# Moving a small norm between the halves of one matmul unit, and a weight split behind two others, in a two-block transformer kernel

## What is computed

```python
# compressed keys of the first attention (nsa)
kc = rms_norm(compress(rope(heads(nkc, G), pos), ...), nsa_kc_norm)   # silu(flat @ w1) @ w2, then norm
vc = compress(heads(nvc, G), cmp_v_pe, cmp_v_w1, cmp_v_w2)
g_nsa = jax.nn.sigmoid(heads(ngate, NSA_HEADS))

# second attention (mla): latents, expanded to queries, keys and values of 8 heads
q_b = (rms_norm(cq, mla_cq_norm) @ w_uq).reshape(B, S, MLA_HEADS, MLA_QK_DIM)
kv_b = (rms_norm(ckv, mla_ckv_norm) @ w_ukv).reshape(B, S, MLA_HEADS, MLA_NOPE_DIM + MLA_V_DIM)
q_b, k_b = rms_norm(q_b, mla_q_norm), rms_norm(k_b, mla_k_norm)       # then rope on the last 64 of 192
```

## Time and profile before

| | |
|---|---|
| median of 3 runs | 1177.66 us (1174.51 to 1179.42) |
| the profiled execution | 1175.0 us, span 1173.7 |
| busy share of the span | TensorE 96%, DVE 64%, ACT 50%, POOL 4% |
| chain that ended last | TensorE 86%, DVE 6%, ACT 4% |
| mean granted TensorE clock | 0.981 of full speed |

### The profile page before, as it was taken

How to read it: one execution, slowest core, us unless ns; L and a number is a source line. 1 busy time by engine, 2 the same in 40 slices (tenths; PEclk the granted TensorE clock), 3 DMA queues, 4 the chain that set the end, 5 groups by cost and what they waited for, 6 DMA issues and landing times.

```text
span 1173.7 us, 19229 instructions
## 1 busy us (share of the span) xinstructions
PE 1126.4 (96%) x7766; PEld 1022.1 (87%) x7766; DVE 755.3 (64%) x1411; ACT 590.5 (50%) x1043; POOL 48.6 (4%) x48
## 2 busy tenths in 40 slices
PE   8999898989899999999998999999999999999998
PEld 7988788888679999888987799998888978999986
DVE  3567486787668778775666666665455566666644
ACT  3365274454556666435344564444465256544542
POOL 0250010000000000101000000000000000000000
PEclk9999899899899999999998999999999999999999
DMA  8954834454135555564632375555544324655450
GB/s 319 390 189 176 339 144 180 154 204 146 40 139 198 183 181 187 215 243 175 235 111 73 119 261 180 179 180 174 185 162 144 108 77 162 204 187 180 131 193 36
DMA packets 30796, 207.81 MB, mean 177 GB/s; under 512 B 3539, under 2 KB 4051, under 8 KB 7156
## 3 DMA queue, kind: packets, MB, share of 16 engines
q1 hardware_dynamic: 30708, 206.58, 49.4%
HBM read 205.52 MB, written 1.05 MB: 176 GB/s over the span
## 4 chain that ended last, share of the span: by engine, by line
PE 86%; DVE 6%; ACT 4%; issue 2%; DMA 1%; SPq 0%; POOL 0%; ACTq 0%; DVEq 0%
PE ps L393 49%; PE ps L1642 19%; PE ps L627 3%; PE ps L411 2%; DVE wlo L352 1%; ACT whi L345 1%; DMA raw<-wa 1%; PE ps L2250 1%; PE ps L2282 1%; PE ps L1340 1%; DVE tm L566 1%; PE ps L816 1%; PE ps L1767 1%; PE ps L1418 1%; PE ps L1142 1%
## 5 line engine op out<-in xcount | busy, mean ns | idle before, releaser
L352 DVE TENSOR_TENSOR wlo<-raw,whi 128x1024 fp32r<-128x1024 f32 (+2 forms) x328 | 372.3, 1177 | 257.1 <-ACT whi L345 256.7
L393 PE MATMUL ps<-H_h,whi 128*128 128x256 f32 x1552 | 446.1, 287 | 0.0
L393 PE MATMUL ps<-H_l,whi 128*128 128x256 f32 x1552 | 440.5, 284 | 0.0
L393 PE MATMUL ps<-H_h,wlo 128*128 128x256 f32 x1552 | 440.5, 284 | 0.0
L345 ACT ACTIVATE whi<-raw 128x1024 fp32r<-128x1024 f32 (+2 forms) x328 | 315.3, 1011 | 176.5 <-PE ps L1642 110.8
L393 PEld LDWEIGHTS ps<-H_h,whi 128*128 128x128 f32 x1552 | 299.4, 193 | 3.9 <-issue 3.3
L393 PEld LDWEIGHTS ps<-H_l,whi 128*128 128x128 f32 x1552 | 299.3, 193 | 0.7 <-issue 0.5
L393 PEld LDWEIGHTS ps<-H_h,wlo 128*128 128x128 f32 x1552 | 299.1, 193 | 0.0
L1642 PE MATMUL ps<-whi,gl_h 128*128 128x512 f32 x264 | 105.6, 400 | 0.5 <-DVE wlo L352 0.5
L1642 PE MATMUL ps<-wlo,gl_h 128*128 128x512 f32 x264 | 104.6, 396 | 0.0
L1642 PE MATMUL ps<-whi,gl_l 128*128 128x512 f32 x264 | 104.6, 396 | 0.0
(11 more groups left out here) (446 smaller groups left out, 1548.9 us busy)
## 6 DMA issues: line engine op xcount, KB each, us to landing
raw<-f SPq DMA_DIRECT2D x44, 1024.0 KB, 4.9
raw<-win SPq DMA_DIRECT2D x27, 1024.0 KB, 5.0
raw<-ada SPq DMA_DIRECT2D x24, 1024.0 KB, 4.9
raw<-up SPq DMA_DIRECT2D x22, 1024.0 KB, 4.8
raw<-g SPq DMA_DIRECT2D x20, 1024.0 KB, 4.9
raw<-pw SPq DMA_DIRECT2D x12, 1024.0 KB, 4.9
raw<-down SPq DMA_DIRECT2D x10, 1024.0 KB, 6.0
raw<-wa SPq DMA_DIRECT2D x4, 1024.0 KB, 10.0
```

Source lines behind the costliest of these rows:

```text
L352: dve.tensor_tensor(wlo[j % NS][:, a:b], raw_of(key)[:, a:b], whi[j % NS][:, a:b].bitcast(F32), ALU.subtract).then_inc(w_lo.hit(key, half), 1)
L393: ins_ = pe.matmul(bank[:, m * 256:(m + 1) * 256], wt[a][:, kt * w + col + m * 128:kt * w + col + m * 128 + 128], act[b][:, k0 + kt, :], s ...
```

## The change

The norm's step on TensorE is issued between the two halves of ("uq", 0) instead of behind both. On ACT it comes behind the copy of the first half, instead of behind that of the second, and on DVE ahead of the gate's two steps and the rotation of `kr`, instead of behind the low split of ("uq", 2). Separately, ACT's and DVE's splits of ("ukv", 1) move from ahead of the hidden layer of the compressed values to behind part 1 of the four parts: on ACT behind the copy of that part, on DVE behind the norm of part 0. One line changes its indentation only.

```diff
@@ latent_pe
                 mm_fm(pe, ("uq", i), cqn, normed("vs") if (i, half) == (0, 0) else held, b, half * 256,
                       done=unit.hit("uq", i) if half else half_done.hit("uq", i))
+                if (i, half) == (0, 0):
+                    key_norm_pe(pe)
...
             if i == 0:
-                key_norm_pe(pe)
                 ada_sums_pe(pe, 8)
@@ latent_act
         for i in range(3):
-            if i == 1:
-                key_norm_act(act)
             if i == 2:
                 cmp_row_act(act, 1)
             next_hi(act, ("uq", i))
...
                 act.activation(dst, v2(where["uq", i, half][:]), ACT.Copy).then_inc(ev_act.hit("uq", i, half), 1)
-        next_hi(act, ("ukv", 0))
+                if (i, half) == (0, 0):
+                    key_norm_act(act)
         hidden_act(act, 1)
...
             act.activation(mk[:, 2 * half:2 * half + 2, :], v2(where["ukv", 0, half][:]), ACT.Copy).then_inc(
                 ev_act.hit("ukv", 0, half), 1)
+            if half == 1:
+                next_hi(act, ("ukv", 0))
         next_hi(act, ("ukv", 1))
@@ latent_dve
         next_lo(dve, ("uq", 0))
+        key_norm_dve(dve)
         dve.wait_ge(*gt_exp())
...
         next_lo(dve, ("uq", 1))
-        key_norm_dve(dve)
         mod_dve(dve, 8)
...
-        next_lo(dve, ("ukv", 0))
         hidden_dve(dve, 1)
         for half in range(4):
             mq_rope_dve(dve, half)
             if half:
                 mq_norm_dve(dve, half - 1)
+            if half == 1:
+                next_lo(dve, ("ukv", 0))
             if half == 2:
                 value_dve(dve)
```

More of the change, by code:

```diff
@@ L1089, in latent_pe @@
                 mm_fm(pe, ("uq", i), cqn, normed("vs") if (i, half) == (0, 0) else held, b, half * 256,
-                      done=unit.hit("uq", i) if half else half_done.hit("uq", i))
+                        done=unit.hit("uq", i) if half else half_done.hit("uq", i))
+                if (i, half) == (0, 0):
+                    key_norm_pe(pe)
             if i == 1:
```

## The result

The changed kernel's median is 1168.48 us (1167.19 to 1171.81, 5 runs) against 1177.66 for the kernel before (1174.34 to 1179.42, 5 runs). The ratio is 0.9947, 95% interval [0.9923, 0.9971]: faster, by 0.3 to 0.8%. The medians lie 9.2 us apart, the means 8.1, and the ratio says 6.2, with an interval of 3.4 to 9.1: five runs each don't tell the gain more closely. The profiled execution took 1167.19 us, span 1165.9, which is 7.8 less than the span of before. The forecast was 1170.1 (1166.1 to 1174.2).

What follows compares the result with a forecast made beforehand. TensorE, busy 96% of the span, was taken to bound the kernel, so only its stalls count. Terms 3.95 + 2.66 + 0.95 = 7.6 us off the median 1177.66 gave 1170.1 us, range 1166.1 to 1174.2.

Steps and rivals of the forecast that it cites:

- Part 1: Norm moved between halves of ("uq", 0): wait ahead of L581 gone, 3.95 us, and slow clock behind it, 2.66 us.
- The split into terms: At L581: 3.95 us idle time, plus 2.66 us slow clock (L581 0.79, L816 0.87, L393 1.00).
- the tightest place: L816 of ("cv1", 2): load landed at 133.0, TensorE comes to it at 133.55, 0.5 us of cover.
- Part 2: Splits of ("ukv", 1) moved: wait ahead of L1142 gone, 1.44 us, less a new wait of 0.5, net 0.95.
- The price at key part 3: Statistics of key part 3: DVE 1.1 us late, so TensorE gets a new wait of 0.5 us.
- the gain comes off either: Whole kernel: the 7.6 us come off the profiled execution, 1175.0, or the median of the runs, 1177.66.
- I see nothing at a fixed time to wait for: Behind the changed stretch: everything is tied to TensorE's progress and loads to buffer read-out, so all follows 7.6 us earlier.
- the prediction's last sign of being wrong: Anywhere in the kernel: the clock falls at a place where it doesn't fall in the kernel before.
- Only the first part pays: Rival: ACT or DVE, carrying the moved split, give its gain back; gain 6.6 us, time 1171.1; chance 0.08.
- The idle time comes back, the clock does not: Rival: at L581 only the idle time is regained; total gain 4.9 us, time 1172.8; chance 0.07.
- The attention stage swallowed nothing: Rival at 220 to 230 us: DVE-bound attention leaves at most some 2 us, 1175.7; chance 0.08 including no effect.
- The slower case: Rival at L816 of ("cv1", 2): load late; landing 20 us after issue gives +7.3, 1185.0; chance 0.03.

Runs made afterwards that it cites:

- filling the wait: Kernel before plus eight matmuls with unread result between L875 and the L581 pair, against the kernel before: timed +2.5 us, ratio 1.0022.
- the repetition: The unaltered changed kernel once more, on the chip that timed the variants, against the kernel before: timed -5.2 us, ratio 0.9957.
- the split only: Kernel before with only both splits of ("ukv", 1) moved behind part 1 of the four parts: timed +2.5 us, ratio 1.0022.
- DVE's step only: Kernel before with only DVE's norm multiply moved, ahead of the low split of ("uq", 2): timed -0.1 us, ratio 0.9998.
- norm on TensorE and ACT only: Kernel before with only TensorE's and ACT's norm steps moved, DVE's multiply left behind the low split: timed +0.1 us, ratio 1.0003.
- norm only: Kernel before with the norm's three steps moved, both splits of ("ukv", 1) left in place: timed -1.6 us, ratio 0.999.

## Why the prediction came out

**Part 1.** The mechanism was as forecast. L875 was forecast at 130.5, `kcn` at 132.2, L581 at 133.1; they came at 130.44, 131.71 to 131.96 and 132.81, all in a run whose stage begins 0.2 earlier. From the 145.58 of L1097 to the 138.84 of L1099 it is 6.74, less those 0.2: 6.5 gained, forecast 6.6. The split into terms held too: filling the wait gave 2.4 of the forecast 2.66, and moving DVE's step alone took away 2.7 us of idle time and the slow stretch with it. The load of ("cv1", 2), the tightest place, landed 6.0 us after its issue and was no wait.

**Part 2.** L1120 to L1120 of parts 0 and 1 is 4.66 us, and the lead grew from 6.75 at the first to 8.29 at the second: 1.5, forecast 1.44. DVE came to the split of ("win", 7) at 162.14, 169.53 less the lead of 8.3 is 161.2, so 0.9 late, forecast 1.1. The price at key part 3 was 0.28 idle and a slower first pair, together 0.5, forecast 0.5. Net 1.0, forecast 0.95. The square on ACT came at 145.59, which is 152.3 less the lead of 6.75, as forecast. What I had left out is that the two parts hang together: with the norm's move alone the second place gets worse by 1.4 us of idle time and a slow stretch, because the load of ("ukv", 1) is not there. I had judged that load only for the new place of its split, where it has the time.

**The sum and the median.** 7.6 in the stage against 7.60 measured. But the step from the stage to the median ("the gain comes off either"; "I see nothing at a fixed time to wait for") is weaker than it looked. There is something that did not follow TensorE's progress in the same way in every execution: where its clock falls. The prediction said that with no idle time the clock has no cause to fall. In the stage it did not fall, but at 407 to 415 us it falls with TensorE busy in every microsecond. By the prediction's last sign of being wrong (the clock falls at a place where it didn't fall in the profile of before) the repetition counts against it: its clock is 0.57 there and 1.00 in the kernel before. The first result gave 0.9947, the repetition 0.9957, some 5 to 6 us. The 7.6 of the stage would be 0.9935: inside the first interval, just outside the second [0.9939, 0.9974]. The first pair of profiles agreed to the tenth of a microsecond, because both executions had the clock falling at the same places of the rest, with 17.4 us lost to it in each.

That the median came so near the 1170.1 is in part luck. The forecast hangs on the median 1177.66 of the first runs of before. Beside the experiments the medians of that kernel were 1173.8 to 1174.0, and less 7.6 that is 1166.2 to 1166.4, 2.3 to 2.6 below the 1168.7 of the repetition; from 1177.66 it is 1170.1, 1.6 above the 1168.5 of the first result. The medians fell by 9.2 us in the first result and by 5.3 in the repetition, around the forecast 7.6 and at neither time by it.

**The rivals.** "Only the first part pays" was wrong both ways: DVE was late as feared but cost 0.5 only, and the first part alone pays little. "The idle time comes back, the clock does not" is refuted for the profile. For the average it stays open, because the slow stretch behind the stall isn't of one size. In the kernel before with two more matmuls the same stall of 3.95 us is followed by 7.66 us from L581 (135.80) to L1097 (143.46), against 8.53 in the profile of before, 8.58 with the split only and 6.03 without a stall: it costs 1.6 and not 2.5. By the Trainium skill (TensorE: Matmul & The Clock Gate, What's actually happening) what watches the activity runs freely beside the kernel. These figures agree with that; no run here shows the watching itself. The attention stage swallowed nothing: TensorE, DVE and ACT took it up at once, with the same busy times in the rest. The slower case, a late load at L816, didn't come, but its twin did in the kernel with the norm's move alone.

**What stays open.** Why the kernel before so often meets the short rest (70 of 79 timed runs lie at 1172.0 to 1176.8, nine at 1177.8 to 1180.6), and with two more matmuls did so in none of six. The spread differs from kernel to kernel too, with a standard deviation of 1.1 us for the split only and for DVE's step only, 2.7 for the changed kernel and 3.1 for the filled wait. The runs show that the rest is longer where the clock is lower, but not what sets where it falls.

## What to carry to other kernels

Look for whose queue a short step waits in before moving the whole chain: one multiply behind a 1.8 us split was 5.1 of the 6.6 us that a stall cost, though the change moved steps on three engines. When a stage gets faster, ask of every load whose reader moves forward with it whether it has landed by then; two moves in one stage may be one move. And measure a small change in its stage, from one instruction to another, since the end-to-end time can answer a small shift by much more: here a delay of 1.1 us cost 6.6. What the stage gains is then still to be confirmed in the timed runs, where only part of it may be left.

## What the runs showed that was not expected

- The time follows the mean granted clock run by run. The five timed runs of the changed kernel: 1167.19 and 1167.21 us at 0.984, 1168.48 at 0.982, 1169.89 at 0.981, 1171.81 at 0.979. So the spread of one kernel, 4.6 us, goes with the clock, and 0.005 of 1167 us is 5.8, enough to make it up. That loads and semaphores add nothing isn't shown.
- In the stage TensorE had the lower clock behind idle times of 3.95 (kernel before), 3.66 (norm on TensorE and ACT only) and 2.73 us (norm only); behind 1.27 and 1.32 us it stayed at 1.00. But idle time ahead is not the whole of it: some 400 us into the rest both kernels of the rows above wait 0.62 us and are then busy without a gap, and in the one with two more matmuls the clock is 1.00 over 583.15 to 590.15 and 0.55 over the busy 590.15 to 597.15, in the kernel before 1.00 throughout.
- Two matmuls that took 1.1 us made the kernel before 6.6 us slower. In its profile the rest is 6.0 longer and has 6.8 us more of lower clock, in stretches 50 to 780 us behind the added matmuls.
